# Requesting the sixth expert's weights after the first two tiles of gathered rows have landed, with a shorter filler before them

## The reference

```python
def hier_moe(h, lp):
    ...
    lg = (x @ lp['router_group_w'] + lp['router_group_b']).astype(F32)
    grp = jnp.argmax(lg, axis=-1)
    ...
    pe, ie = lax.top_k(jax.nn.softmax(le, axis=-1), TOP_K_IN_GROUP)
    ...
    for e in range(N_EXPERTS):
        he = jax.nn.silu(x @ lp['w_gate'][e]) * (x @ lp['w_up'][e])
        y = y + gates[:, e:e + 1] * (he @ lp['w_down'][e])
```

## Time and profile before

| | |
|---|---|
| median of 3 runs | 1030.44 us (1027.97 to 1034.88) |
| profiled execution | 1033.48 us, of which the span from the first to the last instruction is 1031.6 us |
| mean granted TensorE clock | 0.977 |
| PE busy | 948.5 us (92%) |
| DVE / ACT / POOL busy | 439.7 / 316.0 / 281.0 us |
| DMA moved | 212.16 MB, mean 206 GB/s |

### The profile page before, as it was taken

The page is one execution under the profiler, slowest core; times in us unless marked ns, Lnnn a source line. Parts: engine busy times, 40 slices in busy tenths (PEclk is TensorE's granted clock), DMA queues, the critical chain, the costliest instruction groups (busy, mean ns, idle before and its releaser), DMA issues. The chain is left out here.

```text
span 1031.6 us, 21027 instructions
## 1 busy us (share of the span) xinstructions
PE 948.5 (92%) x8032; PEld 614.2 (60%) x8032; DVE 439.7 (43%) x937; ACT 316.0 (31%) x713; POOL 281.0 (27%) x403
## 2 busy tenths in 40 slices
PE   6899999999799989999899999999899999999685
PEld 5456677777566767787455665455455555555341
DVE  2230000002757354677478762447622233333227
ACT  5100000000656323243567642111022232333144
POOL 7000000042100357910356532000223343444113
PEclk9999999999999999999899999999999998999898
DMA  9985642623740038000744253927699999999982
GB/s 302 355 314 220 213 164 86 150 69 101 261 141 7 1 42 195 3 4 13 201 116 132 73 176 138 311 109 295 220 387 382 384 391 383 386 369 370 382 283 99
DMA packets 90506, 212.16 MB, mean 206 GB/s; under 512 B 31730, under 2 KB 54954, under 8 KB 76510
## 3 DMA queue, kind: packets, MB, share of 16 engines
q1 hardware_dynamic: 77666, 187.36, 53.2%
q0 software_dynamic: 9984, 20.15, 6.2%
q10 hardware_dynamic: 2756, 3.27, 0.9%
HBM read 254.83 MB, written 33.95 MB: 280 GB/s over the span
## 5 line engine op out<-in xcount | busy, mean ns | idle before, releaser
L592 PE MATMUL PS<-hT,wring 128*128 128x288 f32 x256 | 83.5, 408 | 0.0
L593 PE MATMUL PS<-hT,wring 128*128 128x288 f32 x256 | 83.0, 406 | 0.0
L2486 POOL DMA_INDIRECT ys_dram<-late,ids x47 | 43.4, 924 | 144.7 <-ACT late L2722 114.7
L2921 DVE COPY mixT<-PS 128x128 f32<-128x128 f32 x49 | 14.3, 292 | 159.6 <-PE PS L2601 159.6
L2480 POOL DMA_INDIRECT mixT<-h_dram,ids x49 | 47.1, 961 | 106.0 <-DVE ids L2888 85.0
L2582 PE MATMUL PS<-ring,mixT 128*64 128x256 f32 x304 | 71.1, 388 | 2.3 <-DVE mixT L2907 2.2
L2583 PE MATMUL PS<-ring,mixT 128*64 128x256 f32 x304 | 71.1, 388 | 0.0
L2582 PEld LDWEIGHTS PS<-ring,mixT 128*64 128x64 f32 x304 | 42.2, 141 | 30.9 <-issue 10.2
L592 PEld LDWEIGHTS PS<-hT,wring 128*128 128x128 f32 x256 | 48.2, 190 | 17.2 <-DVE xc L203 2.6
L593 PEld LDWEIGHTS PS<-hT,wring 128*128 128x128 f32 x256 | 48.6, 190 | 13.4
L2514 PE MATMUL PS<-late,mixT 128*128 128x512 f32 x128 | 55.5, 593 | 0.9 <-PEq L3007 0.9
(11 more groups left out here) (591 smaller groups left out, 2167.7 us busy)
## 6 DMA issues: line engine op xcount, KB each, us to landing
ring<-in_expert_w_gate_dram SPq DMA_DIRECT2D x27, 1024.0 KB
ring<-in_expert_w_up_dram SPq DMA_DIRECT2D x27, 1024.0 KB
ring<-in_expert_w_down_dram SPq DMA_DIRECT2D x27, 1024.0 KB
late<-in_w_ada_dram SPq DMA_DIRECT2D x8, 2048.0 KB
mod_r<-in_expert_w_gate_dram SPq DMA_DIRECT2D x9, 1024.0 KB
mod_r<-in_expert_w_up_dram SPq DMA_DIRECT2D x9, 1024.0 KB
mod_r<-in_expert_w_down_dram SPq DMA_DIRECT2D x9, 1024.0 KB
late<-in_expert_w_gate_dram SPq DMA_DIRECT2D x7, 1024.0 KB
```

The lines of the kernel that those rows point to most:

```text
L592: MM(PS[:, b, 0:HALF], lhs, hT[:, k, 0:HALF], **s)
L593: last = MM(PS[:, b + 1, 0:HALF], lhs, hT[:, k, HALF:NTOK], **s)
L2486: pool.indirect_dma_start(m.ys_dram.ap(), bass.IndirectOffsetOnAxis(ap=ids[:, 1, j:j + 1], axis=0), yr(n), None, bounds_check=LAST_ROW, oo ...
```

## The change

Two edits in `stage_moe`. SP, ahead of the requests for the sixth slot, also waits until the rows of tiles 0 and 1 have landed. And the filler that TensorE runs ahead of `turn(0)` has 21 blocks in place of 33.

```diff
@@ -2415,6 +2415,8 @@
             load_base(4)
             sp.wait_ge(hT_ps, TILES)
             sp.wait_ge(h_out, 16 * TILES)
+            sp.wait_ge(r_in[0], 16)
+            sp.wait_ge(r_in[1], 16)
             load_base(5)
             sp.wait_ge(perm_ok, 1)
 
@@ -2645,7 +2647,7 @@
             logits(PT)
             keep_busy(24)
             counts()
-            keep_busy(33)
+            keep_busy(21)
             pe.wait_ge(te_ok, 1)
             total = pe.value_load(m.te[0:1, 1, 0:1], min_val=0, max_val=NOV)
             turn(0)
```

## The result

The changed kernel takes 1035.95 us in the median of 20 runs (1028.89 to 1038.47), the kernel before 1032.62 us in 20 runs beside it (1027.97 to 1035.98): a ratio of 1.0027, with an interval of 1.0015 to 1.0040. The profiled execution took 1035.06 us, its span is 1033.2 us, the mean clock 0.977 as before.

A forecast was written before the change was run, and what follows sets the result against it. It took the weight stream to set the end, with TensorE having slack: TensorE's 2.6 us gain returns as waiting, the stream moves 0.0, so 1033.5 + 0.0 = 1033.5 profiled, forecast as the median 1030.5; range 1026.3 to 1035.8.

The forecast's parts named there:

- The likeliest case: Expert loop: TensorE starts 2.6 us earlier, the weight stream stays within -1.9 and +1.5 us, end follows weights; chance 0.64.
- the stream's bounds of -1.9 to +3.3: Start of the full weight stream after the sixth slot: at earliest 1.9 us earlier, at latest 3.3 us later.
- the late bound: Tile 1's rows land as before at 738.2, then slot 8.1 us and three gathers 2.1 us: stream 3.3 us later.
- the sum for the stream: Loop's start: landing 736.3, lag 1.65, slot 7.4 and gathers 1.4 us put the stream at 746.75, unmoved.
- The rate: Sixth slot's transfer: 3.15 MB of weights at the full rate in 7.4 us, plus 1.4 us for two gathers.
- The landing: Loop's start: tile 0's rows land 4.0 us after their request, tile 1's at 736.3, when the sixth slot is requested.
- TensorE gains 2.6 us: Loop's start: tile 0's rows land at 734.9, so `turn(0)` and tile 0's products start 2.6 us earlier.
- Waits 9.9 us: Loop's end, 955 to 967: TensorE waits 9.9 us for weights in place of 7.3.
- 1.4 and 0.8 us idle, the same picture: TensorE around `turn(0)`: idle pieces of 1.4 and 0.8 us, the clock falling as before at the same price, 2.6 us earlier.
- the rows were not held by the weights: Rival at the loop's start: rows land as before, TensorE gains nothing, stream begins 3.3 us later, 1033.8 us; chance 0.16.
- turns between the queues: DMA engines alternate queues by packet: a gather beside weights loses only 0.69 us, and freeing the way gains `turn(0)` 0.7 us.
- The lead lasts: Rival at the loop's end: it follows TensorE, not the stream, so 2.6 us stay gained, 1027.8 us; chance 0.13.

The follow-up runs named there:

- e9: Changed kernel with the sixth slot's w_gate requested where it was before, w_up and w_down still behind the rows, third chip: ratio to the kernel before 0.9995.
- e12: The changed kernel itself, unmodified, run again on a third chip: ratio to the kernel before 1.0036 (1.0009 to 1.0064).
- e11: Changed kernel with the sixth slot's request also waiting for tile 1's products, third chip: ratio to the kernel before 1.0080 (1.0048 to 1.0112).
- e3: Changed kernel with the sixth slot's w_gate requested where it was before, w_up and w_down still behind the rows, first chip: ratio to the kernel before 0.9951.
- e5: The changed kernel itself, unmodified, run again on a second chip: ratio to the kernel before 1.0005 (0.9981 to 1.0030).
- e10: As e9, with three filler pieces of 512 columns for TensorE ahead of its wait for own_ok: ratio to the kernel before 0.9987 (0.9958 to 1.0015).
- e6: The kernel before itself, unmodified, run again on a second chip: 1034.2 us.
- e7: Kernel before, loading only 16 of 128 partitions of three experts' w_down, second chip: ratio to the kernel before 0.9971 (0.9947 to 0.9995).
- e8: Kernel before with two filler matmul pieces ahead of the products of each of tiles 12 and 16, second chip: ratio to the kernel before 1.0006 (0.9981 to 1.0032).
- e1: Changed kernel with the filler back at 33 blocks, so only the new wait, first chip: ratio to the kernel before 0.9981 (0.9955 to 1.0006).
- e2: Kernel before with only the filler cut from 33 to 21 blocks, first chip: ratio to the kernel before 0.9986 (0.9958 to 1.0014).
- e4: Changed kernel with the sixth slot's requests also waiting for tile 0's products, first chip: ratio to the kernel before 0.9953 (0.9927 to 0.9978).

## Why the prediction held, and which term was off

The likeliest case was right in its mechanism: TensorE gains, the hole in the stream moves to the front, and the end follows the weights (shown by e9 against e12 and by e11; the shown pair alone does not show the last step). The ratio of 1.0027 puts it at 1033.2 us on the scale of the 1030.44 that I started from, inside the range, and the 2.8 us are inside the stream's bounds of -1.9 to +3.3. (The median itself, 1035.95, is 0.15 us above the range's end, because the kernel before also came out 2.2 us higher over 20 runs than over three.) Its first number, no change, was wrong: it is a small loss. The case was also given more narrowly, a stream moved by -1.9 to +1.5 us with a chance of 0.64, and 1.7 us by the windows, 2.8 by the ratio, is past that. The range held because it was wide, with 3.3 us for the late bound and 2 us more for the scatter between executions. The step that failed is the sum for the stream, "The stream proper begins at ... 746.75 ... So 0.0 us".

- **The rate.** I let the slot's 3.15 MB pass at the full rate in 7.4 us and gave the gathers 1.4 us. In 738 to 748 the changed kernel's engines were full and moved only 3.23 MB. Its queues in that stretch:

```profile
q1 hardware_dynamic: 364, 2.72, 84.7%
q0 software_dynamic: 242, 0.50, 17.7%
```

The weights themselves were slow: 2.72 MB in 8.5 us of the engines' time is 321 GB/s, against 425 in rows 8, which would have been 6.4 us. So they lost 2.1 us, and the gathers took 1.8 us in place of 1.4: 2.5 us together. The same 10 us after t0 in e3, e5, e9, e10 and e12 have 313 to 336 GB/s for the weights beside 0.47 to 0.53 MB on the gathers' queue. In e11, where the slot's transfer met only 0.17 MB of that in 10 us, the weights had 3.64 MB in 9.0 us, 403 GB/s. That points to gathers as what slows weights beside them; no run was made to test it.
- **The landing.** The rows landed sooner than I said: `turn(0)` 3.1 us after the request and not 4.0, the slot requested at 735.7 and not 736.4. This gave 0.6 us back. 2.5 less 0.6 is 1.9 us, and the windows have 1.7.
- **The execution that I read.** The trace of before had tile 0 at half clock, and its first freed slot was requested 14.2 us after t0. Three others with the same code at that place have 11.2 to 12.6. Against the mean of stream positions of e6, e7, e8 and the shown one (+0.4 MB) the changed kernel's three traces (-0.5 MB) are 0.9 MB behind, 2.3 us, which is the measured 2.8 within its interval. I took the clock's fall to be the same before and after; the one before was worse than usual and made the hole look wider.
- **TensorE's side.** "TensorE gains 2.6 us": 3.3 to 3.7 us by the traces; the first freed slot, expected to be requested at 742.5, was at 740.3. "Waits 9.9 us": 9.5, 9.4 and 7.9. "1.4 and 0.8 us idle, the same picture" for the clock: the idle piece ahead of `turn(0)` was 0.54 us and the clock stayed up through tile 0. It fell afterwards, in 743 to 748 (0.66 in the mean), behind the 2.16 us wait for DVE that the prediction did not look for. The stream was full by then.
- **Edit 2** is needed for the first one to show in full: with 33 blocks `turn(0)` came at 5.0 us and not 3.1 (e1). Alone it does harm to the stream (e2).

The rivals: "the rows were not held by the weights" is refuted by 3.0 us to landing in place of 6.6, and with it the idea that turns between the queues leave a gather nearly untouched. What the Trainium skill says of turns ("DMA: Bandwidth & Descriptors", "Queues, rings and completion order") isn't what rows 8 and this landing look like. The advice of the Trainium skill to issue a DMA early (the same page, "Rules for kernel authors") is borne out by e9 (1.0036 to 0.9995 with 1 MB issued early) and e11 (1.0080 with 3 MB issued late). "The lead lasts" is refuted for the runs on record. But it was dismissed too lightly: the two bounds are within some microseconds of each other. In all four traces of the first chip TensorE waited for no weights, at ends of 303 to 307.5 us after t0, and there e4, 1.2 MB behind, was faster than the kernel before (0.9953). Whether the change itself gains on such a chip was not measured; e1 and e2, each with one edit, are within noise there. Why TensorE waited 9.8 to 10.7 us at the tiles without products (the line named in e1) on that chip and 2.9 to 3.1 us in all other traces is open, and with it whether it is the chip.

The version that keeps the rows' early landing and the stream's position (e3, e9, e10) is ahead of the changed kernel on the one chip where both ran. Against the kernel before it is faster on one chip (0.9951, interval clear of 1) and the same on the other (0.9995, 0.9987 with the filler). On the first chip e4 did as well (0.9953); over both chips it is the best of those tried.

## What to carry to other kernels

When a transfer is moved behind another to clear its way, ask where the hole that it filled goes: with a saturated stream afterwards, what is moved out of an idle stretch is paid for at about the stream's rate (here 3.3 to 3.8 MB cost 8.4 us), unless the compute engine is the one that ends last; then it costs nothing (e4). Move only as much as gets in the way; here 1 MB of 3 fitted in front of the gathers at no cost to them. And read such a margin from more than one execution, since with a fall of the clock the kernel before requested its first freed slot 1.6 us later than without (14.2 against 12.6 us after t0), about as much as the change lost.

## What the runs showed of the hardware

- A gather of 64 rows requested while 3 MB of weights were under way on another queue moved nothing for some 3 us and landed after 6.6 us (rows 7 and 8); with empty engines it landed after 3.0 us (changed kernel).
- DMA engines that are shown as full (1.03) can move 300 to 347 GB/s or 425: a share of 1.0 is no rate.
- Waits at the same tiles without products were 2.9 to 3.1 us in ten traces, those of two chips and the shown pair, and 9.8 to 10.7 us in the four traces of a third chip, all of variants of the kernel (e1 to e4).
- In the eight traces in which the loop waited for weights, 63.7 to 65.3 us followed the last such wait, whatever the variant.
